# Gate sums of all DeltaNet heads fetched as rows from DRAM, key norms taken by ScalarE, and a head's first steps moved up by one projection step

## The reference

```python
q = l2_normalize(q) * DK_B ** -0.5          # x * rsqrt(sum(x * x) + 1e-6), over 128 channels
k = l2_normalize(k)
gcum = jnp.cumsum(gc, axis=-1)              # gate sums inside a chunk
diff = gcum[..., :, None] - gcum[..., None, :]
decay = jnp.where(tril, jnp.exp(jnp.where(tril, diff, 0.0)), 0.0)
lower = jnp.tril(jnp.einsum('...id,...jd->...ij', kb, kc) * decay, -1)
a_mat = lower + jnp.eye(c)
sol = lax.linalg.triangular_solve(a_mat, rhs, left_side=True, lower=True, unit_diagonal=True)
attn = jnp.einsum('...id,...jd->...ij', qc, kc) * decay
```

## Time and profile before

| | us |
|---|---|
| median of 3 runs | 2000.53 |
| lowest, highest | 1999.17, 2001.12 |
| the profiled execution | 2001.81 |
| its span | 2000.0 |
| TensorE busy in it | 1962.6 (98%) |
| VectorE, ScalarE, POOL busy | 1234.6, 733.6, 670.3 |

### The profile page before, as it was taken

The page is one execution under the profiler, slowest core; times in us unless marked ns, Lnnn a source line. Parts: engine busy times, 40 slices in busy tenths (PEclk is TensorE's granted clock), DMA queues, the critical chain, the costliest instruction groups (busy, mean ns, idle before and its releaser), DMA issues.

```text
span 2000.0 us, 37378 instructions
## 1 busy us (share of the span) xinstructions
PE 1962.6 (98%) x15596; PEld 1902.4 (95%) x15596; DVE 1234.6 (62%) x2460; ACT 733.6 (37%) x1268; POOL 670.3 (34%) x659
## 2 busy tenths in 40 slices
PE   6999999999999999999999999999999999999997
PEld 4999999999999988889999999999999999999997
DVE  6666566756663435665433389999999954563334
ACT  5422222232222124544212255555555543352220
POOL 4123212311320222002211158888888840031110
PEclk9999999999999999999999999999999999999998
DMA  5221222112222234112344333333332322223333
GB/s 195 75 64 56 65 66 64 65 56 64 66 70 89 94 139 162 54 54 77 121 132 132 108 107 91 89 95 95 96 95 87 86 75 85 85 91 120 101 105 113
DMA packets 79721, 184.14 MB, mean 92 GB/s; under 512 B 26776, under 2 KB 35928, under 8 KB 79304
## 3 DMA queue, kind: packets, MB, share of 16 engines
q1 hardware_dynamic: 72304, 166.22, 27.2%
q0 software_dynamic: 3504, 9.63, 1.4%
q10 hardware_dynamic: 3744, 5.90, 0.8%
HBM read 162.66 MB, written 19.06 MB: 91 GB/s over the span
## 4 chain that ended last, share of the span: by engine, by line
PE 86%; DVE 10%; issue 1%; POOL 1%; ACT 1%; DMA 0%; SPq 0%; POOLq 0%; DVEq 0%; ACTq 0%
PE acc L580 71%; DVE arena L1551 2%; DVE full L1554 2%; PE acc L654 2%; DVE w_lo L1551 2%; PE gp L778 1%; DVE act_lo L1551 1%; PE acc L682 1%; POOL small L2295 1%; PE gp L788 1%; PE gp L884 1%; PE gp L770 1%; PE gp L936 1%; DVE full L1551 1%; PE gp L766 1%
## 5 line engine op out<-in xcount | busy, mean ns | idle before, releaser
L580 PE MATMUL acc<-act_hi,w_hi 128*128 128x288 f32 x3904 | 861.2, 302 | 0.3 <-DVE w_lo L1551 0.3
L580 PE MATMUL acc<-act_hi,w_lo 128*128 128x288 f32 x3904 | 836.4, 296 | 0.0
L580 PE MATMUL acc<-act_lo,w_hi 128*128 128x288 f32 x3904 | 835.4, 296 | 0.0
L580 PEld LDWEIGHTS acc<-act_hi,w_hi 128*128 128x128 f32 x3904 | 625.2, 189 | 14.7 <-issue 9.5
L580 PEld LDWEIGHTS acc<-act_hi,w_lo 128*128 128x128 f32 x3904 | 628.9, 189 | 0.0
L580 PEld LDWEIGHTS acc<-act_lo,w_hi 128*128 128x128 f32 x3904 | 627.9, 189 | 0.0
L2295 POOL TENSOR_TENSOR arena<-arena 128x512 f32<-128x512 f32 (+2 forms) x281 | 386.9, 1377 | 348.0 <-ACT arena L1397 284.1
L1093 ACT ACTIVATE w_hi<-w_raw 128x1024 fp32r<-128x1024 f32 x264 | 277.1, 1054 | 416.0 <-PE acc L580 309.9
L1551 DVE TENSOR_TENSOR w_lo<-w_raw,w_hi 128x1024 fp32r<-128x1024 f32 x264 | 382.4, 1468 | 41.3 <-ACT w_hi L1093 40.4
L1554 DVE SCALAR_TENSOR_TENSOR gp<-arena,par,gp 128x64 f32<-128x64 f32 (+1 forms) x688 | 248.0, 441 | 0.0
L1093 ACT ACTIVATE arena<-arena,par 128x512 f32<-128x512 f32 x240 | 165.1, 720 | 95.6 <-POOL arena L2295 88.0
(11 more groups left out here) (263 smaller groups left out, 1784.0 us busy)
## 6 DMA issues: line engine op xcount, KB each, us to landing
w_raw<-wt SPq DMA_DIRECT2D x264, 512.0 KB, 4.0
full<-x SPq DMA_DIRECT2D x16, 288.0 KB, 6.9
arena<-x SPq DMA_DIRECT2D x16, 288.0 KB, 3.7
arena<-x_scratch SPq DMA_DIRECT2D x16, 288.0 KB, 2.8
x_scratch<-full ACTq DMA_DIRECT2D x14, 288.0 KB, 3.9
out_y<-full SPq DMA_DIRECT2D x24, 144.0 KB, 1.9
arena<-state_in SPq DMA_DIRECT2D x6, 512.0 KB, 4.1
out_sdn<-arena POOLq DMA_DIRECT2D x6, 512.0 KB, 3.1
```

Source lines behind the costliest of these rows:

```text
L580: ins = pe.matmul(acc[:, s, i, 0:HALF], w[:, s, wk], a[:, k, i * HALF:(i + 1) * HALF], start=(k == 0 and j == 0), stop=(k == KT - 1 and j ...
```

## The change

Three things are done.

The running gate sums no longer come from POOL's `gB` and TensorE's `gcum` in every head. Four matmuls in the preparation compute the sums of all eight heads at once, with the 8 heads on the partitions. VectorE copies them to SBUF, POOL stores them to DRAM (`gate_rows`, 8 x 512), and for every head POOL issues a transfer that reads one row of 2 KB into all 128 partitions, at step 9 of the head before (the first one in the preparation). `dmask` waits for that transfer.

The squares of k are no longer taken channel-major and summed by TensorE. ScalarE squares the transposed k out of PSUM, with its accumulated output giving the sum per token (`ksq`, four instructions of 128 x 128, behind `kv_tok`). `sq` squares q alone (512 wide), `norm` has four matmuls, and `ssum` becomes two instructions, of which the first takes ScalarE's sums.

Without gcum, `norm` stands behind step 2 and `gram` behind step 3. `kg` moves behind `attn`. POOL's steps up to `L4` and VectorE's up to `X` move up by one.

```diff
-PE_HEAD = (["kv_tok", "gcum", "norm", "gram"] + [f"{s}{i}" for i in LV for s in ("a", "x")]
+PE_HEAD = (["kv_tok", "norm", "gram"] + [f"{s}{i}" for i in LV for s in ("a", "x")]
...
-PE_PLAN = {1: "kv_tok", 2: "gcum", 3: "norm", 4: "gram"}
-PE_PLAN |= {11 + i: n for i, n in enumerate(PE_HEAD[4:-1])}
+PE_PLAN = {1: "kv_tok", 2: "norm", 3: "gram"}
+PE_PLAN |= {11 + i: n for i, n in enumerate(PE_HEAD[3:-1])}
...
-ACT_PLAN = {1: ["sq"], 2: ["decay"]} | {PE_AT[f"a{i}"]: [f"A{i}"] for i in LV}
+ACT_PLAN = {1: ["sq", "ksq"], 2: ["decay"]} | {PE_AT[f"a{i}"]: [f"A{i}"] for i in LV}
...
-DVE_PLAN = {1: ["kg"], 2: ["dmask"], 3: ["ssum"], 4: ["vs", "Mt", "attn"], 6: ["mc", "solve", "Xt", "X"]}
+DVE_PLAN = {2: ["dmask", "ssum"], 3: ["vs", "Mt", "attn", "kg"], 5: ["mc", "solve", "Xt", "X"]}
...
-POOL_PLAN = {0: ["scalars", "gB"], 3: ["nrm", "rn", "bn", "bp"], 4: ["B"], 7: ["L3"], 8: ["L4"]}
+POOL_PLAN = {0: ["scalars"], 2: ["nrm", "rn", "bn", "bp"], 3: ["B"], 6: ["L3"], 7: ["L4"]}
...
+    g_dram = nc.dram_tensor("gate_rows", (H, SEQ), F32, kind="Internal").ap()
...
+                for c in range(NC):
+                    pe.matmul(gp[0:H, 2, c * P:(c + 1) * P], gates[:, :, KG, c], tri, start=True, stop=True)
                 pe.matmul(gp[:, 1, 0:32], tri, gk, start=True, stop=True)
...
-                elif name == "gcum":
-                    pe.wait_ge(pool_h.sem, pool_h.at("gB", it))
-                    for c in range(NC):
-                        ins = pe.matmul(gp[:, 2, ck(c)], gB[:, c, :], tri, start=True, stop=True)
                 elif name == "norm":
                     pe.wait_ge(act_h.sem, act_h.at("sq", it))
-                    for c in range(8):
-                        ins = pe.matmul(gp[:, 3, c:c + 1], sqkq_c[:, c, :], ones[:, 0:1], start=True, stop=True)
+                    for c in range(NC):
+                        ins = pe.matmul(gp[:, 3, c:c + 1], q_sq[:, ck(c)], ones[:, 0:1], start=True, stop=True)
...
-                    ins = act.activation(sqkq, kqv[kb][:, 0:2, :], ACT.Square)
+                    ins = act.activation(q_sq, kqv[kb][:, 1, :], ACT.Square)
+                elif name == "ksq":
+                    act.wait_ge(pe_h.sem, pe_h.at("kv_tok", it))
+                    for c in range(NC):
+                        ins = act.activation(k_sq[:, c, :], gp[:, 0, c * P:(c + 1) * P], ACT.Square,
+                                             accum_out=ksum[:, c:c + 1])
                 elif name == "decay":
+                    act.wait_ge(pool_h.sem, pool_h.at("scalars", it))
                     act.wait_ge(dve_h.sem, dve_h.at("dmask", it))
...
+                dve.tensor_copy(g_turned, gp[0:H, 2, :])
...
                 elif name == "dmask":
-                    pe_at("gcum")
-                    ins = tt(dec, bank4(2), per_group(negm, 4), ADD)
+                    dve.wait_ge(g_in, 16 * (it + 1))
+                    ins = tt(dec, g_row, per_group(negm, 4), ADD)
                 elif name == "ssum":
                     pe_at("norm")
-                    ins = ts(ssum, gp[:, 3, 0:8], EPS, None, ADD)
+                    dve.wait_ge(act_h.sem, act_h.at("ksq", it))
+                    ts(ssum[:, 0:4], ksum, EPS, None, ADD)
+                    ins = ts(ssum[:, 4:8], gp[:, 3, 0:4], EPS, None, ADD)
...
+            def gate_row(it):
+
+                row = g_dram[it].unsqueeze(0).to_broadcast([P, SEQ])
+                pool.dma_start(g_row, row.rearrange("p (c t) -> p c t", t=P)).then_inc(g_in, 16)
...
-                elif name == "gB":
-                    own("scalars")
-                    ins = copy(gB, per_row(hs[:, KG, 0:4], P))
...
+                            if 8 * ti + e == 9 and it < H - 1:
+                                pool.wait_ge(dve_h.sem, dve_h.at("dmask", it))
+                                gate_row(it + 1)
...
+                        if hp == 0 and (ti, e) == (3, 2):
+                            pool.wait_ge(prep, 3)
+                            pool.dma_start(g_dram, g_turned).then_inc(g_stored, 16)
+                        if hp == 0 and (ti, e) == (3, 6):
+                            pool.wait_ge(g_stored, 16)
+                            gate_row(0)
```

More of the change, by code:

```diff
@@ L104 @@
 assert LEVELS == 7
-DVE_HEAD = (["kg", "dmask", "ssum", "vs", "Mt", "attn", "mc", "solve", "Xt", "X"]
+DVE_HEAD = (["dmask", "ssum", "vs", "Mt", "attn", "kg", "mc", "solve", "Xt", "X"]
             + [n for i in LV for n in [f"X{i}"] + [f"T{i}"] * (i in IN_BLOCKS)]
@@ L108 @@
             + ["on", "y"])
-ACT_HEAD = ["sq", "decay"] + [f"A{i}" for i in LV] + [f"q{c}" for c in range(1, NC)] + ["osq"]
-POOL_HEAD = (["scalars", "gB", "nrm", "rn", "bn", "bp", "B"] + [f"L{i}" for i in LV]
+ACT_HEAD = ["sq", "ksq", "decay"] + [f"A{i}" for i in LV] + [f"q{c}" for c in range(1, NC)] + ["osq"]
+POOL_HEAD = (["scalars", "nrm", "rn", "bn", "bp", "B"] + [f"L{i}" for i in LV]
              + ["f1", "f2", "f3", "f4", "f5"])
-PE_PLAN = {1: "kv_tok", 2: "gcum", 3: "norm", 4: "gram"}
-PE_PLAN |= {11 + i: n for i, n in enumerate(PE_HEAD[4:-1])}
+PE_PLAN = {1: "kv_tok", 2: "norm", 3: "gram"}
+PE_PLAN |= {11 + i: n for i, n in enumerate(PE_HEAD[3:-1])}
 def counts(names):
@@ L292, in hybrid_step @@
         mtl = [fa[:, 1024 + 512 * i:1536 + 512 * i].rearrange("p (c t) -> p c t", t=P) for i in range(2)]
-        gB = fa[:, 2048:2560].rearrange("p (c t) -> p c t", t=P)
+        g_row = fa[:, 2048:2560].rearrange("p (c t) -> p c t", t=P)
+        g_turned = arena[0:H, 10364:10876]
         x_d, a1_d = (fa[:, 2560 + 256 * i:2816 + 256 * i].rearrange("p (c t) -> p c t", t=HP2) for i in range(2))
@@ L297, in hybrid_step @@
         diagonal = (lower, upper)
-        sqkq = fa[:, 3584:4608].rearrange("p (s t) -> p s t", s=2)
-        sqkq_c = fa[:, 3584:4608].rearrange("p (s c t) -> p (s c) t", s=2, t=P)
+        q_sq = fa[:, 3584:4096]
+        k_sq = fa[:, 4096:4608].rearrange("p (c t) -> p c t", t=P)
         o_sq = fa[:, 4096:4608].rearrange("p (c t) -> p c t", t=P)
@@ L327, in hybrid_step @@
         eps_p2 = tiny(8)
+        ksum = tiny(4)
         mh = mhalf
         x_in = [[sem(f"x_in{a}_{i}") for i in range(8)] for a in range(2)]
+        g_stored, g_in = sem("gate_rows_stored"), sem("gate_row_in")
         wab_in, wab_scaled, ident_in = sem("wab_in"), sem("wab_scaled"), sem("ident_in")
```

## The result

| | before | changed |
|---|---|---|
| median, us | 2000.76 (4 runs) | 1981.7 (4 runs) |
| lowest, highest | 1999.17, 2001.12 | 1979.13, 1984.83 |
| the profiled execution, its span | 2001.81, 2000.0 | 1979.13, 1977.3 |

The forecast was 1982.7 us. The same kernel run again on another occasion gave 1985.37 us (first experiment), so the true value lies a little above 1981.7, and the forecast between the two.

What follows compares the result with a forecast made beforehand. The prediction took TensorE's instruction stream (86% of the span) as the bound. 14.2 removed, less 0.8 added, plus 2.0 and 2.4 of lateness gave 17.8 us less: 2000.5 to 1982.7 us, range 1980.2 to 1988.

Steps and rivals of the forecast that it cites:

- gcum and half of norm: TensorE matmuls removed in eight heads: gcum saves 7.3 us, half of norm 6.9 us, together 14.2 us.
- The preparation: Four matmuls added once on TensorE behind the gate mask sums: 0.8 us, ends 0.5 and 1.2 us.
- kv_tok's lateness: TensorE's wait at kv_tok for y, behind silu slowed beside gB, goes away: 2.0 us, low end 0.
- a3's lateness: TensorE's wait for X at the first solve matmuls goes as gram moves up: 2.4 us, low end 1.
- The new waits: ssum's wait for ksq and dmask's for the gate row, all costed at nothing.
- The sum: Whole kernel: 14.2 - 0.8 + 2.0 + 2.4 = 17.8 us less.
- From the sum to the time: 17.8 us off the profiled execution gives 1984.0 us; off the median, 1982.7 us.
- item on the clock: A 1.2 GHz stretch behind the sampled norm's one-column matmuls may go or a second come: 1.7 us either way.
- (a): Rival: only the removed matmuls count, the latenesses at kv_tok and a3 stay; 1987.1 us, chance 0.12.
- (b): Rival: gram waits for ssum, ksq ending 1.5 us later; 0.6 us per head, 4.8 us, 1987.5 us; chance 0.06.
- (c): Rival: nothing won, the time returns as lateness at o_chan or the weights; about 1999 us, chance 0.03.
- (d): Rival: POOL's B, L3, L4 hold VectorE up between Mt and X, a3 2.65 us late per head; 2006.3 us, chance 0.03.

Runs made afterwards that it cites:

- rows_only: Kernel before with only the gate rows through DRAM (gcum and gB out, preparation matmuls in), norm and gram steps unmoved; 1993.99 us, ratio 0.9964.
- ksq_only: Kernel before with only the key norms by ScalarE (norm with four matmuls, kg behind attn), gB and gcum kept; 1994.8 us, ratio 0.9967.
- copy_back: Changed kernel plus a POOL copy of 128 x 512 where gB stood, into memory nobody reads, without gcum; 1985.61 us, ratio 0.9932.
- fill_three: Changed kernel plus three POOL memsets of 128 x 512, one behind the other, where gB stood; 1982.35 us, ratio 0.9912.
- unmoved: Changed kernel with norm and gram, and VectorE's and POOL's steps for them, put back one projection step later; 1988.16 us, ratio 0.9936.
- after_again: Changed kernel without an edit, timed and profiled once more; 1985.37 us, ratio 0.9918 to the kernel before.
- row_at_kv_tok: Changed kernel with each head's own gate row (but the first) fetched only when its kv_tok is done; 1992.7 us, ratio 0.9957.
- fill_back: Changed kernel plus one POOL memset of 128 x 512 where gB stood; 1982.07 us, ratio 0.9915.
- row_step31: Changed kernel with the next head's gate row fetched at step 31 of the head before, not step 9; 1984.13 us, ratio 0.9915.
- o_chan_later: Changed kernel with o_chan one step later, directly ahead of kv_tok, and into PSUM bank 2; 1980.71 us, ratio 0.9906.

## Why the prediction was right

- **gcum and half of norm, 14.2 us.** Predicted 7.3 and 6.9. rows_only and ksq_only bear the two out separately: 6.4 of the 8.0 us of the one, and the 6.1 us of the other, in seven distances. Right because the cost was read as a distance between starts, not as a duration. Half of norm is 0.89 us a head, not 0.86, so 7.1 in all: the 0.03 kept back for a group's fixed cost does not show.
- **The preparation, 0.8 us.** 0.98 measured: the small stationary tile saves nothing against gcum's 0.91 for four. Within the bounds (0.5 to 1.2).
- **kv_tok's lateness, 2.0 us.** Gone in all heads. copy_back brings it back with a POOL copy like gB alone, and fill_three, with as long a stretch of writing in the same place, doesn't: it hung on POOL reading SBUF beside silu.
- **a3's lateness, 2.4 us.** Gone, and of that size: of the 0.93 and 7 x 0.31 us over the pitch, 0.09 each was not lateness, which leaves 0.84 + 7 x 0.22 = 2.4. The cause was right, but that the size fits is luck: 2.4 was the middle between 1.6 and 3.2, and the 0.09 were not known. unmoved keeps the lateness, so it was the move that took it away. The margin is 14.52 - 13.15 = 1.4 us, 1.2 less the 0.15 for the signal, where 1.1 was announced: the chain from gram to X grew by 0.05 us and not by 0.1, since kg filled the time in which the split used to be held.
- **The new waits, nothing.** Right for ksq (with K for kv_tok's start again, 0.25 us from one square to the next, the four over at K + 2.1, before norm ends at K + 3.4) and for the rows. Wrong in a detail: the first row was to be there by 89.4 and came at 91.2, since the store was issued at 81.9 and not at 80. From there store and fetch took 9.2 us, as the 2 x 4.7 said. Mt of head 0 starts at 102.7, so there were over 11 us to spare.
- **The sum.** From head 0's kv_tok in the prompt to the first step of the sampled part it was 548.57 us and is 529.74, 18.8 less, against 14.2 + 2.0 + 2.4 = 18.6. With the preparation's 0.98 the saving is 17.8 us, as forecast; the 0.2 us too little for norm and the 0.2 too little for the preparation cancel.
- **From the sum to the time.** 1984.0 was due for the profiled execution, and it took 1979.1. From the first step of the sampled part to the end it is 5.9 us shorter than before, by no clock fall there (1.7 us) and a stretch in which projections ran faster (4 us, below); the start is 1.0 us longer beyond the preparation's matmuls. after_again, the same kernel, has the fall and not the fast stretch, so neither belongs to the change. That the median came out within 1 us of the forecast is in part luck too, given 1981.7 and 1985.37 for one kernel. In its item on the clock the prediction counts 32 one-column matmuls; those are records, two to a matmul, so 16 matmuls.

Of the rivals, (a) was that the latenesses stay: unmoved and copy_back are what that looks like, for one of them each. (b) needs a gate row or a sum that comes 1.3 us later: row_at_kv_tok made it so, and gram did wait. (c) and (d) did not show: TensorE's waits have no new entry and its waits for a3 and kv_tok are gone, and X, for which a3 was 0.2 us late in most heads, is there 1.4 us ahead.

## What to carry to other kernels

Where one engine is busy 98% of the time, count what leaves its stream by the distance between starts, and then look for its small latenesses: here two of 0.2 to 0.4 us a head made a quarter of the gain, and each had its cause on another engine. The one went with the operation that held that engine up, the other because its chain was given one more step. A fetch that is issued early costs nothing until its landing passes the instruction queued behind the waiting one. When an edit saves a few tenths of a per cent, measure it over the repeated part of the trace; the whole time scatters by more than that.

## What the runs showed of the hardware that was not expected

**TensorE at 130 ns in place of 133.3.** In some executions the projection matmuls run 2.5% faster for 160 to 360 us, at a granted clock of 1.00 all the time. The same window, first of the changed kernel's profiled execution, then of after_again's (in brackets the matmuls):

```profile
960.00:1080.00 120.00, 120.00 (x925) 120.00 (x924) 39.96 (x29) 26.72 (x30) 12.79 (x9) 1.00 0.41 127
```

```profile
960.00:1080.00 120.00, 120.00 (x902) 120.00 (x901) 38.57 (x27) 25.32 (x28) 12.90 (x9) 1.00 0.40 129
```

In after_again they stand 133.3 ns apart from start to start, in the changed kernel's first profile 130.0. It comes at other places in other executions: 937 to 1102 us here, 1772 to 1933 in fill_back, from 1162 to 1173 on until 1502 to 1534 in unmoved, row_step31, row_at_kv_tok and fill_three, nowhere in the other six. Why is open.

**And it is given back where VectorE is the bound.** Between 1164 and 1507 us (layer 1) VectorE is busy 94 to 97% of the time. One window of it in fill_three, and then the longest wait of TensorE behind it:

```profile
1240.00:1320.00 80.00, 80.00 (x618) 80.00 (x617) 77.68 (x172) 46.25 (x63) 70.99 (x55) 1.00 0.36 92
```

```profile
PE acc L585 <- DVE arena L1563: 7.6, 1, 7.6
```

TensorE gains about 9 us there (some 2640 matmuls from 1164 to 1507 us, 3.3 ns each), then waits 7.6 us for VectorE in one piece, to 1571.4. In after_again, without a fast stretch, the same wait is 1.4 us, and in the changed kernel's first profile there is none. So that part of layer 1 has hardly any slack on VectorE's side. That an edit which saved TensorE time in that stretch would win little is what this suggests; no run here tried it.

**The clock falls at varying places.** All twelve profiled executions have the lower level, 1.2 GHz, in their last 10 to 13 us. Besides that it falls for 3.4 us at 629 to 650 us (the kernel before, rows_only, ksq_only, copy_back, o_chan_later, row_at_kv_tok), near 1630 (after_again, fill_back, and 6.8 us in o_chan_later), and nowhere else in the changed kernel's first profile. Each of the 3.4 us falls begins 0.2 to 1.6 us after a run of one-column matmuls has ended, 16 of them at the first place and 12 at the second. But both runs stand in every kernel here, and the clock stays up behind the first in six executions of twelve and behind the second in nine, so they alone do not decide it. The longest, 6.8 us in fill_three and 10.2 in unmoved, row_step31 and row_at_kv_tok, begin while TensorE stands still in the wait of 7.6 us that fill_three's row just showed (in row_step31 it waits from 1566.1 to 1573.6, and the clock falls at 1568.8). So a fast stretch is paid for there a second time.

**The start scatters.** kv_tok of the first head stands at 93.2 to 95.9 us in the ten profiled executions whose TensorE has the same work up to there (all but the kernel before and ksq_only, which lack the four matmuls of the preparation). The two ends are row_at_kv_tok and the changed kernel, which are alike in all they do up to there. The start, the fast stretches and the clock are large enough to make the medians of one kernel differ by 3.7 us; since only one execution of each run was profiled, it is not shown that they do.
